# One more slot of dense work in "forget", and pairs of units in the second block's self-attention

## Reference

```python
def forgetting_attention(q, k, v, log_f):          # first block, 4 heads of 64, both layers
    c = jnp.cumsum(log_f, axis=1)
    ...
    s = jnp.einsum('bqhd,bkhd->bhqk', qn, k) * scale + cqn[..., None] - c_keys   # causal
    p = jax.nn.softmax(s, axis=-1)
    return jnp.einsum('bhqk,bkhd->bqhd', p, vf)    # then times silu(za)

def diff_attention(q1, q2, k1, k2, v, lam, bias_dist):   # second block, 4 heads, layer 0
    a = probs(qa, k1) - lam * probs(qc, k2)        # two causal softmaxes with a bias by distance
    return jnp.einsum('bhqk,bkhd->bqhd', a, v)     # heads of 128; then rms_norm, pool, w_out
```

## Time and profile before

| | |
|---|---|
| time, median of 3 runs | 2230.22 us (2229.02 to 2235.14) |
| time of the profiled execution | 2231.92 us |
| its span (first to last instruction) | 2230.1 us |
| PE busy | 2206.0 us, 99% |
| weight loads of PE busy | 1865.7 us, 84% |
| DVE busy | 1454.6 us, 65% |
| ACT busy | 974.9 us, 44% |
| mean granted clock of PE | 0.995 |

### The profile page before, as it was taken

How to read it: one execution, slowest core, us unless ns; L and a number is a source line. 1 busy time by engine, 2 the same in 40 slices (tenths; PEclk the granted TensorE clock), 3 DMA queues, 4 the chain that set the end, 5 groups by cost and what they waited for, 6 DMA issues and landing times.

```text
span 2230.1 us, 31738 instructions
## 1 busy us (share of the span) xinstructions
PE 2206.0 (99%) x12112; PEld 1865.7 (84%) x12112; DVE 1454.6 (65%) x2448; ACT 974.9 (44%) x1676; POOL 14.5 (1%) x14
## 2 busy tenths in 40 slices
PE   9999999999999999999999999999999999999998
PEld 7877788888778888888898889998888888899997
DVE  5866665557656566586765677776755656776775
ACT  5444533333545344364554544443322434444444
POOL 0000000000000000200000000000000000000000
PEclk9999999999999999999999999999999999999999
DMA  5555443335644323455354333333333313233331
GB/s 200 177 160 165 148 128 107 105 125 169 180 140 148 126 94 116 131 162 151 109 147 144 102 92 97 104 99 100 95 95 95 95 48 100 90 104 95 97 113 55
DMA packets 136694, 268.14 MB, mean 120 GB/s; under 512 B 21773, under 2 KB 79931, under 8 KB 136160
## 3 DMA queue, kind: packets, MB, share of 16 engines
q1 hardware_dynamic: 136544, 266.13, 38.9%
HBM read 235.37 MB, written 26.77 MB: 118 GB/s over the span
## 4 chain that ended last, share of the span: by engine, by line
PE 72%; DVE 2%; ACT 1%; issue 1%; POOL 0%; DMA 0%; DVEq 0%; POOLq 0%; SPq 0%; ACTq 0%
PE ps L2114 22%; PE ps L2116 22%; PE ps L2115 22%; PE ps L2142 1%; PE ps L2131 1%; POOL t_UP L2097 0%; PE ps L2166 0%; PE ps L2156 0%; PE ps L2154 0%; PE ps L2168 0%; PE ps L2155 0%; PE ps L2167 0%; DVE t_wlo L2430 0%; ACT t_Tb L2338 0%; DVE t_Tb L2658 0%
## 5 line engine op out<-in xcount | busy, mean ns | idle before, releaser
L2114 PE MATMUL ps<-t_P0H,t_whi 128*128 128x512 f32 (+1 forms) x1568 | 590.9, 377 | 2.0 <-DVE t_P0L L2475 1.0
L2115 PE MATMUL ps<-t_P0L,t_whi 128*128 128x512 f32 (+1 forms) x1568 | 584.5, 373 | 0.0
L2116 PE MATMUL ps<-t_P0H,t_wlo 128*128 128x512 f32 (+1 forms) x1464 | 552.9, 378 | 0.0
L2430 DVE TENSOR_TENSOR t_wlo<-t_raw,t_whi 128x1024 fp32r<-128x1024 f32 (+2 forms) x289 | 342.6, 1186 | 46.7 <-PE ps L2116 34.4
L2257 ACT ACTIVATE t_whi<-t_raw 128x1024 fp32r<-128x1024 f32 (+2 forms) x295 | 300.5, 1024 | 163.8 <-PE ps L2116 162.4
L2114 PEld LDWEIGHTS ps<-t_P0H,t_whi 128*128 128x128 f32 x1568 | 295.3, 188 | 72.1 <-issue 15.9
L2115 PEld LDWEIGHTS ps<-t_P0L,t_whi 128*128 128x128 f32 x1568 | 294.9, 188 | 56.2 <-issue 1.0
L2116 PEld LDWEIGHTS ps<-t_P0H,t_wlo 128*128 128x128 f32 x1464 | 275.2, 188 | 54.7
L2114 PE MATMUL ps<-t_P1H,t_whi 128*128 128x512 f32 (+1 forms) x548 | 210.1, 383 | 2.3 <-DVE t_P1L L2815 1.0
L2115 PE MATMUL ps<-t_P1L,t_whi 128*128 128x512 f32 (+1 forms) x548 | 208.4, 380 | 0.0
L2116 PE MATMUL ps<-t_P1H,t_wlo 128*128 128x512 f32 (+1 forms) x524 | 201.0, 384 | 0.0
(11 more groups left out here) (348 smaller groups left out, 3896.6 us busy)
## 6 DMA issues: line engine op xcount, KB each, us to landing
t_raw<-in_wts SPq DMA_DIRECT2D x362, 512.0 KB, 3.6
far<-t_Tb SPq DMA_DIRECT2D x26, 384.0 KB, 2.8
far<-t_Tb SPq DMA_DIRECT2D x16, 512.0 KB, 3.1
t_PTX<-far SPq DMA_DIRECT2D x64, 96.0 KB, 3.3
t_raw<-in_wts SPq DMA_DIRECT2D x16, 384.0 KB, 3.1
t_QKV<-far SPq DMA_DIRECT2D x32, 128.0 KB, 2.8
t_raw<-in_wts SPq DMA_DIRECT2D x13, 256.0 KB, 2.9
t_PTX<-far SPq DMA_DIRECT2D x24, 128.0 KB, 2.6
```

Source lines behind the costliest of these rows:

```text
L2114: e.matmul(s.out, s.sh, s.mh, start=s.first, stop=False, skip_group_check=again)
L2115: e.matmul(s.out, s.sh, s.ml, start=False, stop=False, skip_group_check=again)
L2116: i = e.matmul(s.out, s.sl, s.mh, start=False, stop=s.end, skip_group_check=again)
L2430: e.tensor_tensor(s.dst, s.raw, s.hi.bitcast(F32), ALU.subtract).then_inc(*mark("lo", s.j))
```

## The change

```diff
@@ attention, twos
                 for u in now:
                     scores(u)
                 if apart:
+                    if not now:
+                        yield
+                        flush()
                     values(old[1])
@@ first block, both layers
-        phase("forget", tok, 2, qA, kA, vA, [0, 1], [0, 1], gens_B(tokB), 90, 15, M[:, 4:6, :], M[:, 6:8, :])
+        phase("forget", tok, 2, qA, kA, vA, [0, 1], [0, 1], gens_B(tokB), 90, 16, M[:, 4:6, :], M[:, 6:8, :])
@@ second block, before its self-attention
-    SB.idle += PTP.idle
-    PTP.idle = []
+    SB.idle += PTP.idle + OB.idle[1:]
+    PTP.idle, OB.idle = [], OB.idle[:1]
@@ second block, its self-attention
-    drive(attention(eun, head_done, twos=False), fill_E(), 116, 30, lead=2)
+    drive(attention(eun, head_done), fill_E(), 116, 30, lead=2)
+    OB.idle, SB.idle = OB.idle + SB.idle[:1], SB.idle[1:]
     early.append(wo_E(2))
```

## The result

The changed kernel takes 2237.56 us (median; 2234.99 to 2240.76), the kernel before, run beside it, 2234.12. The ratio is 1.002, with a 95% interval from 1.0012 to 1.0027: 0.2% slower, within the 0.3% that counted as no change. The forecast was 2219.6, or 0.5% faster, in a range of 2212 to 2228. Its direction and its range were both wrong.

The account below looks back on a forecast made before the run. PE, 99% busy, was taken to bound the kernel, leaving only waits and slow-clock stretches to gain. First block -11.8 us and second +1.2 made -10.6: 2219.6 us against the median 2230.22, range 2212 to 2228.

Parts of the forecast that it names:

- What bounds the kernel; a wait costs its length and half of the slow stretch.: PE, 99% busy: an edit gains only its waits plus half of the 1.2 GHz stretches behind them.
- The slot removes gate_y's wait, with no wait left.: First block's forget, both layers: a slot between values(u2) and values(u3) removes the stall, gaining 11 to 12.1, taken as 11.8 us.
- The shorter rounds (22 to 24 steps instead of 24) take 1.4 us at most from chains that show no wait.: First block's forget: 90 steps over 16 slots shorten rounds, costing chains without waits at most 1.4 us.
- need not stand at all: Second block, before step 26: lower bound of PE's new wait, 2.5 us, if DVE does not stand for u1's far transfer.
- The new wait at step 26: 4.4 us, bounds 2.5 and 4.7, and a slow stretch.: Second block: PE waits 4.4 us instead of 0.8 for a query weight's low half, plus 1.7 us of slow clock.
- values(u3) on the head's copy: 0.4, and nothing for head 3.: Second block, one output bank: values(u3) waits 0 to 0.9, taken as 0.4 us, for head 0's copy; head 3's first unit nothing.
- All 5.3 us of the stage's own losses go.: Second block: waits of 0.8, 1.4 and 1.4 us and 1.7 us of slow clock all removed.
- the forecast of +1.2: Second block with two units at once: 6.5 us added, 5.3 removed, net 1.2 us lost, between 5.3 gained and 8.5 lost.
- The lent bank removes no wait.: Second block: the lent bank removes no wait, as no score on PE waits for a bank in the list.
- Takes back most of it: Rival, chance 0.15: second block removes none of the 5.3 us and adds 8.5, giving -3.3 us, 2227.
- Slower than before: Rival, chance 0.05: copies queue on DVE, values(u3) and values(u9) cost about 6 us each atop 8.5, giving +8.7, 2239.
- What would show it.: Signs of failure: L2142 still waits on L2603 (gate_y), or the second block's stage changes by more than 8 us.

Follow-up runs that it names:

- the two kernels without the loan: Changed kernel with 15 shares, two output banks and three for scores, two or six steps ahead in second block: +4.5 and +2.5 us against the kernel before.
- the late transposition: Near-side transposition put behind the exponents on DVE; in the second block of the changed kernel with 15 shares: -12.1 us against the kernel before.
- part 2 alone: Kernel before with pairs of units, the lent output bank and the slot in the second block only, first block unchanged: 2238.71 us, +5.6 us.
- the slot alone: Kernel before with the slot added in the first block, the 90 steps still over 15 shares, second block unchanged: 2223.77 us, ratio 0.9954.
- 16 shares and late transposition: Kernel before with the first block's slot, 16 shares, three steps ahead, and transpositions behind exponents in forget: 2226.03 us, ratio 0.9968.
- single visits and late transposition: Kernel before with the first block's slot, 15 shares, one unit a visit and transpositions behind exponents in the second block: 2219.61 us, ratio 0.9937.
- with pairs (at 940.87): Changed kernel with 15 shares and transpositions behind exponents in the second block: 2219.85 us, ratio 0.9946 against the kernel before.
- the spread alone: Kernel before with the first block's 90 steps spread over 16 shares and no slot added: 2237.68 us, ratio 1.0020.
- part 1 alone: Kernel before with the slot and 16 shares in the first block, second block unchanged: 2231.36 us, ratio 0.9995.

## Why the prediction was wrong, point by point

- *What bounds the kernel; a wait costs its length and half of the slow stretch.* Right: PE's busy time is unchanged, and in the changed kernel PE's waits grew by 7.1 of the 8.0 us by which its span did; the two kernels without the loan lost time in a third place, score products that overlap less.
- *The slot removes gate_y's wait, with no wait left.* Right: gate_y starts at 116.28, values(u3) at 119.84 without idle time. Mis-sized by little: 9.0 to 10.3 us measured with 15 shares, against 11.8.
- *"The shorter rounds (22 to 24 steps instead of 24) take 1.4 us at most from chains that show no wait."* **This is the step that failed.** It priced the spread by the length of a round and read the absence of a wait as slack. It didn't list, for each step that lets go of a weight, on which side of a round's boundary it falls before and after. It even had the new boundary, "48 steps instead of 51", so that steps 49 to 51 change sides. Step 49 crossed it, its low half came 10 us later against the stage's start (39.6 us after the first scores before, 92.45 less 52.88; 49.9 after, 103.58 less 53.64) where it had 5.8 us of slack, and the loss was about 9 us of 10. I had done this listing for step 73, and for step 25 in the second block, but not for the rest.
- *DVE "need not stand at all".* The stand for the far transfer was in the sum of the second block as a time of arrival, and absent from the first. With the late transposition it turned out to be what both losses had in common: that order alone gave back 6 us in each block.
- *The new wait at step 26: 4.4 us, bounds 2.5 and 4.7, and a slow stretch.* The mechanism was right in each link; the size was 5.4 (5.05 to 5.37 in three kernels), over the upper bound. u0's transposition alone stood 2.22 us instead of 0.84, which the working took over from before unchanged.
- *values(u3) on the head's copy: 0.4, and nothing for head 3.* Mis-sized: 1.6 to 1.7, and 1.1 at head 3's first unit too. The copy at 980.99 began 2.4 us after its products had ended (978.54), behind two evictions and a low half on DVE; the row I had taken, of another head, began 1.6 us after them, behind one low half.
- *All 5.3 us of the stage's own losses go.* Half right: the weight wait with its slow stretch near 1024 is gone, as forecast, and the 0.8 at step 26 went into the new wait. The wait of 1.4 for the norm's column is not gone; there are two now, 1.0 and 1.1.
- These three terms (1.0, 2.4 and, with 1.4 not gone and 0.8 more, 2.2) make 5.6 us over the forecast of +1.2; measured was +5.6 in all, 4.4 over. The stage gave about 1 us back elsewhere, which I can't place.
- *"The lent bank removes no wait."* Wrong for pairs, though the sum didn't use it: it was read from the list of single visits, and without the loan the pairs are 10 us slower.
- *The rivals.* "Takes back most of it" had the second block nearly right (it lost 5.6 of the 8.5 allowed) with the first block's gain kept; no rival had the spread in it. That was the gap in the list. "Slower than before" comes near in number (2239) by luck: it has values(u3) and values(u9) cost some 6 us each, and they wait 1.7 and 1.1 us.
- *What would show it.* Neither sign of failure came: no value product waits for gate_y, and the second block's stage changed by 5.5 us (part 2 alone), under the 8. No sign looked at forget ahead of gate_y, where the loss was.
- *The DMA estimate.* The page "DMA: Bandwidth & Descriptors" of the Trainium skill gives the 2.0 us in its section on DMAs that GpSimd issues; the DMAs here are issued by SyncE. Nothing in the sum hung on it.

So the miss of 15 us (forecast -10.6, measured +4.5) is some 9 us of the spread, 4.4 us of the second block and 1.5 us of the slot.

## What to carry to other kernels

When a change re-spreads filler work over slots, list for every releasing step the slot it falls in before and after, and what stands ahead of its follow-up on the in-order engine; "no wait is shown" says nothing of slack. Look for instructions that stand at the head of a queue for a DMA round trip, and put ready work in front of them first: here that gave 4 to 6.5 us in three kernels and needs no new resource, while pairs and lead steps gave nothing. Work run ahead of a stage is no gift: in one kernel here it was taken from the cover inside it.

## What the runs showed of the hardware that was not expected

- **A wait's length doesn't tell whether the clock falls.** Waits of 1.43 us before (at 1023.55), 2.00 us with the slot alone (at 1015.67) and 1.85 us with 16 shares and late transposition (at 101.45) each stand beside a stretch at 0.50. Waits of 1.80 us with single visits and late transposition (at 1011.26) and of 2.17 us with pairs (at 940.87) have none, nor have waits of 2.37 and 2.43 us with the spread alone (at 116.02 and 543.57). The wait of 1.43 us has a twin in the kernel with part 1 alone, at the same place in the program (1.86 us, at 1023.57), without a stretch.
- **Nor does it tell how long the clock stays down.** Behind the same wait at step 26 it stood at 0.50 for 3.4 us after 5.37 us of idle time and for 6.8 us after 5.05. The page "TensorE: Matmul & The Clock Gate", Part 1, of the Trainium skill says of the slow matmuls at a kernel's start that their number varies from run to run, and warns against fitting to a count; these rows, from the middle of a kernel, vary too.
- **The waits themselves repeat closely.** The wait at step 26 was 5.37, 5.34 and 5.05 us in three kernels with the same order in that stage, and those of forget with the slot and 16 shares 4.40 and 3.94, 3.42 and 3.20 in two. So one trace each can compare orders whose waits differ by more than half a microsecond, but not their time, of which the clock has a part.
